# Expert weights w1 read as rows of 32 KB in two transfers of 4 MB, instead of 16 KB rows in four of 2 MB

## What is computed

```python
logits = (x @ router_w + router_b).astype(jnp.float32)
top_vals, top_idx = lax.top_k(logits, TOP_K)            # 4 of 32
gates = jax.nn.softmax(top_vals, axis=-1)
h = x_pad[tok] @ w1[e] + b1[e]                          # 1024 -> 2048
out = clamped_swiglu(h) @ w2[e] + b2[e]                 # 1024 -> 1024
out = out * row_gate[:, None]                           # then added per token
```

## Time and profile before

| | |
|---|---|
| Median of three runs | 1197.25 us (1196.84 to 1197.47) |
| Profiled execution, device time | 1195.7 us |
| Its span, first to last instruction | 1193.9 us |
| Mean granted TensorE clock | 0.963 |
| TensorE matmul busy | 1078.5 us (90%) |
| VectorE, ScalarE, GpSimd busy | 281.6, 184.7, 92.6 us |
| Moved by DMA | 429.84 MB, mean 360 GB/s |

### The profile page before, as it was taken

The page is one execution under the profiler, slowest core; times in us unless marked ns, Lnnn a source line. Parts: engine busy times, 40 slices in busy tenths (PEclk is TensorE's granted clock), DMA queues, the critical chain, the costliest instruction groups (busy, mean ns, idle before and its releaser), DMA issues.

```text
span 1193.9 us, 13476 instructions
## 1 busy us (share of the span) xinstructions
PE 1078.5 (90%) x4855; PEld 428.3 (36%) x4856; DVE 281.6 (24%) x648; ACT 184.7 (15%) x373; POOL 92.6 (8%) x133
## 2 busy tenths in 40 slices
PE   5983898999999999999999998899989998999996
PEld 4752445333333333333333333333333333333332
DVE  2997713411112111111111111111111111111112
ACT  3550611011111111111111111111111111111112
POOL 0690000000000000000000000000000000000000
PEclk9996888799999999999999999999999999999999
DMA  9800945199999996999999999999999999999981
GB/s 313 310 28 0 294 160 233 64 384 428 427 427 427 427 428 244 428 425 427 429 427 427 428 427 427 427 428 428 428 426 428 427 427 429 428 428 425 428 358 44
DMA packets 43979, 429.84 MB, mean 360 GB/s; under 512 B 6191, under 2 KB 13767, under 8 KB 19364
## 3 DMA queue, kind: packets, MB, share of 16 engines
q1 hardware_dynamic: 40492, 421.10, 84.9%
q0 software_dynamic: 3328, 8.17, 1.8%
q10 hardware_dynamic: 144, 0.38, 0.1%
HBM read 430.29 MB, written 4.62 MB: 364 GB/s over the span
## 4 chain that ended last, share of the span: by engine, by line
PE 48%; DMA 41%; DVE 8%; ACT 1%; issue 1%; SPq 0%; DVEq 0%; ACTq 0%
DMA W<-in_w_dram 41%; PE PS L926 16%; PE PS L947 15%; DVE WA L1017 3%; DVE WA L1014 3%; PE PS L811 3%; PE PS L649 2%; PE PS L918 2%; PE PS L682 1%; PE PS L645 1%; PE PS L638 1%; DMA WA<-in_state_conv_dram 1%; PE PS L620 1%; PE PS L632 1%; PE PS L867 1%
## 5 line engine op out<-in xcount | busy, mean ns | idle before, releaser
L947 PE MATMUL PS<-W,XT 128*64 128x512 f32 x1056 | 249.2, 615 | 51.4 <-DMA W<-in_w_dram 47.6
L926 PE MATMUL PS<-WB,X 128*64 128x512 f32 x1088 | 236.3, 592 | 0.0
L926 PE MATMUL PS<-WA,X 128*64 128x512 f32 x1024 | 222.4, 592 | 0.0
L1217 DVE TENSOR_SCALAR X<-PS 128x512 f32<-128x512 f32 x33 | 22.8, 691 | 607.1 <-PE PS L926 607.1
L947 PEld LDWEIGHTS PS<-W,XT 128*64 128x64 f32 x1056 | 74.7, 140 | 179.1 <-issue 122.9
L926 PEld LDWEIGHTS PS<-WB,X 128*64 128x64 f32 x1088 | 78.1, 137 | 155.3 <-issue 155.3
L926 PEld LDWEIGHTS PS<-WA,X 128*64 128x64 f32 x1024 | 73.5, 137 | 146.7 <-issue 146.7
L591 ACT ACTIVATE X<-X 128x512 f32<-128x512 f32 x33 | 20.8, 630 | 482.0 <-DVE X L1217 482.0
L1333 POOL COPY gcol<-stab 128x1 uint32 x33 | 6.0, 182 | 879.9 <-PE PS L638 879.9
L1204 DVE TENSOR_TENSOR X<-PS,par 128x512 f32<-128x512 f32 x34 | 23.5, 691 | 198.5 <-PE PS L638 198.5
L649 PE MATMUL PS<-XT 64*128 64x512 f32 x272 | 67.6, 615 | 0.0
(11 more groups left out here) (242 smaller groups left out, 657.8 us busy)
## 6 DMA issues: line engine op xcount, KB each, us to landing
WA<-in_w_dram SPq DMA_DIRECT2D x64, 2048.0 KB, 25.8
WB<-in_w_dram SPq DMA_DIRECT2D x64, 2048.0 KB, 25.2
W<-in_w_dram SPq DMA_DIRECT2D x64, 2048.0 KB, 24.7
WB<-in_w_in_dram SPq DMA_DIRECT2D x5, 1024.0 KB, 12.0
WB<-in_w_in_dram SPq DMA_DIRECT2D x1, 2048.0 KB, 14.7
W<-in_w_out_dram SPq DMA_DIRECT2D x1, 2048.0 KB, 18.4
W<-in_w_out_dram SPq DMA_DIRECT2D x2, 1024.0 KB, 9.8
h_rows<-M POOLq DMA_DIRECT2D x3, 512.0 KB, 7.5
```

What stands on the lines that cost most here:

```text
L926: last = mm(PS[64 * n:64 * n + 64, s, :], xTe[:, o:o + SLOTS], w1buf[u][:, c, q:q + 512], start=False, stop=(c == 3 and k == 1))
L947: last = mm(PS[64 * n:64 * n + 64, MIX, :], hT[:, s, h, :], w2buf[:, 4 * h + s, 512 * n:512 * n + 512], start=(s == 0 and h == 0), stop=(s ...
```

## The change

w1 is read with four neighbouring rows per partition, so a chunk has 32 KB in one run on each partition and there are two chunks of 4 MB per expert. Everything that depends on it follows: two semaphores for arrival and two for release, the order of the 64 matmuls of a block (two chunks of 32), the columns that the transposes read (every fourth element in place of every second), the layout of the router's weights, and the norm's gains, which come in one transfer of two rows and are turned by four small transposes in place of two. The first loads of the weights are cut otherwise: of w1 of expert 1, 4 MB are issued early in place of 6 MB, and 4 MB later in place of 2 MB. The bytes are the same.

```diff
-        w1buf = [WA[:, :].rearrange("p (c n) -> p c n", c=4),
-                 WB[:, :].rearrange("p (c n) -> p c n", c=4)]
+        w1buf = [WA[:, :].rearrange("p (c n) -> p c n", c=2),
+                 WB[:, :].rearrange("p (c n) -> p c n", c=2)]
...
-        w1_v = w1.rearrange("l e (c p k) n -> p (l e) c (k n)", p=P, k=2)
+        w1_v = w1.rearrange("l e (c p k) n -> p (l e) c (k n)", p=P, k=4)
...
-                (gain_rows[0:2, :], ffn_norm_g[0].rearrange("(h c n) -> h c n", h=2, c=2)[:, 0, :]),
-                (gain_rows[2:4, :], ffn_norm_g[0].rearrange("(h c n) -> h c n", h=2, c=2)[:, 1, :]),
+                (gain_rows, ffn_norm_g[0].rearrange("(h n) -> h n", h=2)),
...
-            o = 256 * chunk_of(k) + k // 4
-            return slice(o, o + 255, 2)
+            o = 512 * (k % 2) + k // 2
+            return slice(o, o + 509, 4)
...
-            load_w1(sp, 0, 0, range(2))
+            load_w1(sp, 0, 0, range(1))
...
-            load_w1(sp, 1, 1, range(3))
+            load_w1(sp, 1, 1, range(1))
...
-            load_w1(sp, 0, 0, range(2, 4))
-            load_w1(sp, 1, 1, range(3, 4))
+            load_w1(sp, 0, 0, range(1, 2))
+            load_w1(sp, 1, 1, range(1, 2))
...
-                    for c in range(4):
+                    for c in range(2):
                         sp.wait_ge(w1_used[c], end)
                         load_w1(sp, u, 2 * i + u + 2, [c])
...
-                    o = 256 * (k % 2) + k // 2
-                    last = tp(PS[:, LIN, P * k:P * k + P], xg[:, o:o + 255:2], ident)
+                    last = tp(PS[:, LIN, P * k:P * k + P], xg[:, k:k + 509:4], ident)
...
-            for k in range(2):
-                tp(PS[:, 7, 20 + 4 * k:24 + 4 * k], gain_rows[:, k::2], ident[0:4, 0:4])
+            for k in range(4):
+                tp(PS[:, 7, 20 + 2 * k:22 + 2 * k], gain_rows[:, k::4], ident[0:2, 0:2])
...
-                        for c in range(4):
+                        for c in range(2):
                             pe.wait_ge(w1_in[u][c], 16 * i + 16)
-                            for k in range(2):
-                                o = SLOTS * (4 * k + 2 * (c % 2) + c // 2)
+                            for k in range(4):
+                                o = SLOTS * (2 * k + c)
                                 for s in range(2):
                                     for n in range(2):
                                         q = 2048 * k + 1024 * s + 512 * n
                                         last = mm(PS[64 * n:64 * n + 64, s, :], xTe[:, o:o + SLOTS],
-                                                  w1buf[u][:, c, q:q + 512], start=False, stop=(c == 3 and k == 1))
+                                                  w1buf[u][:, c, q:q + 512], start=False, stop=(c == 1 and k == 3))
                             last.then_inc(w1_used[c], 1)
...
-                    dve.wait_ge(w1_used[3], m + 1)
+                    dve.wait_ge(w1_used[1], m + 1)
```

More of the change, by code:

```diff
@@ L170, in hybrid_step @@
         par_rows = c3[0:20, 3584:3712]
-        gain_rows = c3[0:4, 3712:3968]
+        gain_rows = c3[0:2, 1280:1792]
         q_sb = c3[:, 0:1280].rearrange("p (g t) -> p g t", g=G)
@@ L263, in hybrid_step @@
         kv_in, q_in, wout_in, wout2_in = (sem(n) for n in ("kv_in", "q_in", "wout_in", "wout2_in"))
-        w1_in = [[sem(f"w1_in{u}{c}") for c in range(4)] for u in range(2)]
+        w1_in = [[sem(f"w1_in{u}{c}") for c in range(2)] for u in range(2)]
         w2_in = [sem("w2_in0"), sem("w2_in1")]
@@ L278, in hybrid_step @@
         xg_ready, pool_step, xtp_ready, xT_ready = sem("xg_ready"), sem("pool_step"), sem("xtp_ready"), sem("xT_ready")
-        w1_used = [sem(f"w1_used{c}") for c in range(4)]
+        w1_used = [sem(f"w1_used{c}") for c in range(2)]
         g_ready, sig_ready = sem("g_ready"), sem("sig_ready")
@@ L293, in hybrid_step, with load_w1 @@
         nv_sv = nv_s[0].rearrange("b w h d -> b w (h d)")
-        def load_w1(eng, u, e, chunks=range(4)):
+        def load_w1(eng, u, e, chunks=range(2)):
             for c in chunks:
@@ L318, in rows_of @@
         def rows_of(k):
-            o = 256 * chunk_of(k) + k // 4
-            return slice(o, o + 255, 2)
-        def chunk_of(k):
-            return 2 * (k % 2) + k // 2 % 2
+            o = 512 * (k % 2) + k // 2
+            return slice(o, o + 509, 4)
         def Hs(i):
@@ L370, in _ @@
             sp.dma_start(sinks8, attn_sinks[0].partition_broadcast(P)).then_inc(caches_in, 16)
-            sp.dma_start(rw[:, :, :].rearrange("p (c k) e -> p c (k e)", k=2),
-                         router_w[0].rearrange("(c p k) e -> p c (k e)", p=P, k=2)).then_inc(late_in, 16)
+            sp.dma_start(rw[:, :, :].rearrange("p (c k) e -> p c (k e)", k=4),
+                         router_w[0].rearrange("(c p k) e -> p c (k e)", p=P, k=4)).then_inc(late_in, 16)
             sp.dma_start(rb[:, :], router_b[0].partition_broadcast(P)).then_inc(late_in, 16)
             sp.dma_start(b1q[:, :], b1[0].rearrange("e (q n) -> (e q) n", n=512)).then_inc(b1_in, 16)
-            load_w1(sp, 0, 0, range(2))
+            load_w1(sp, 0, 0, range(1))
             sp.dma_start(wout[:, G:KD, :], w_out[0, 512:1024, :].rearrange("(j p) n -> p j n", p=P)).then_inc(wout2_in, 16)
@@ L427, in _ @@
                 if e < E - 2:
-                    for c in range(2):
-                        sp.wait_ge(w1_used[c], end)
-                        load_w1(sp, e % 2, e + 2, [c])
+                    sp.wait_ge(w1_used[0], end)
+                    load_w1(sp, e % 2, e + 2, [0])
                 if e == E - 3:
@@ L435, in _ @@
                 if e < E - 2:
-                    for c in range(2, 4):
-                        sp.wait_ge(w1_used[c], end)
-                        load_w1(sp, e % 2, e + 2, [c])
+                    sp.wait_ge(w1_used[1], end)
+                    load_w1(sp, e % 2, e + 2, [1])
                 if e in (E - 4, E - 2):
@@ L631, in router @@
                 for k in range(KD):
-                    last = nc.tensor.matmul(PS[:, 1, E * i:E * i + E], hTr[:, k, :], rw[:, 2 * chunk_of(k) + k // 4, :], start=(k == 0), stop=(k == KD - 1))
+                    last = nc.tensor.matmul(PS[:, 1, E * i:E * i + E], hTr[:, k, :], rw[:, 4 * (k % 2) + k // 2, :], start=(k == 0), stop=(k == KD - 1))
                 last.then_inc(S["lg_done"], 1)
@@ L653, in _ @@
             pe.wait_ge(consts_in, 16)
-            pe.wait_ge(rows_in, 16 * 8)
+            pe.wait_ge(rows_in, 16 * 7)
             tp(PS[:, 7, 0:20], par_rows, ident[0:20, 0:20])
-            for k in range(2):
-                tp(PS[:, 7, 20 + 4 * k:24 + 4 * k], gain_rows[:, k::2], ident[0:4, 0:4])
+            for k in range(4):
+                tp(PS[:, 7, 20 + 2 * k:22 + 2 * k], gain_rows[:, k::4], ident[0:2, 0:2])
             for j in range(CJ):
```

## The result

The changed kernel took 1199.55 us (median of 9 runs, 1198.87 to 1201.51) against 1197.47 for the kernel before on the same chip (9 runs, 1195.79 to 1199.42). The ratio is 1.0021, with a 95% interval from 1.0011 to 1.0031: 1.3 to 3.7 us slower. The profiled execution has a span of 1197.2 us, 3.3 more than that of before.

What follows compares the result with a forecast made beforehand. Weight transfers set the pace except before two restarts of an idle queue. Terms 3.5 + 0.3 - 1.0 + 3.5 - 3.2 = +3.1 us gave 1200.3 us on the median, range 1196.8 to 1204.9.

Steps and rivals of the forecast that it cites:

- the five stretches: Start to first w1 release, seven experts' transfers, TensorE to the next release, 22 experts' transfers, two blocks; each counts in full.
- the front: Before the expert loop: two more small transposes of the gains stand ahead of the other transposes on TensorE, +0.3 us.
- The two releases: At both queue restarts w1 is released after 32 matmuls in place of 16: 3.5 us each, +7.0 us together.
- The cover behind the restart: Right behind a restart the next w1 issue has 2.4 us in hand, so the coarser release is hidden there.
- The rows of 32 KB: In w1 transfers, one 32 KB packet replaces two of 16 KB, sparing 9 ns: -1.0 and -3.2 us, -4.2 together.
- The sign of being wrong: Prediction wrong if the queue idles anywhere else, or the long stretch's slope moves by more than 0.5%.
- packets as before: Rival: rows are cut at 16 KB or priced by bytes, so only releases and front count: +7.3, 1204.6 us; chance 0.22.
- cheaper rows: Rival: 32 KB rows and fewer transfers spare more than the line says, 1196.1 or 1197.7 us, not slower; chance 0.16.
- Fewer, larger transfers: Two transfers fewer per expert on SyncE's queue: at most 2.6 us spared, taken as nothing.
- the last rival: Something at a restart or the end: a slow group, 1.7 us, or another start, 1 or 2 us either way; chance 0.08.
- Moved early loads: 2 MB of expert 1's w1 move from the issue near 121 us to that at 167, 8 us in hand: 0.
- reads at stride four: Transposes' loads at stride four cost no more than at stride two, judged from line 938: 0.

Runs made afterwards that it cites:

- the coarse release alone: Kernel before, with w1 chunks issued in pairs after 32 matmuls in place of 16, 16 KB rows and layout kept: 1204.12 us, ratio 1.0052.
- one-block pair: Kernel before and changed kernel, each with one block for every expert, the crowded expert's tokens past 64 left out: 1185.37 and 1185.03 us.
- the layout alone: Changed kernel's layout, strides and gains, but transfers, releases and early loads as in the kernel before: 1198.32 us, ratio 1.0000.
- the 8 KB rows: Changed kernel, but each w1 chunk comes in two 2 MB transfers with 8 KB runs, release still after 32 matmuls: 1213.15 us, ratio 1.0127.
- the only version here: Changed kernel's layout, first w1 chunk in two 2 MB transfers with 16 KB runs, second in one with 32 KB runs: 1197.28 us, ratio 0.9988.

## Why the prediction was right

**What bounds the kernel.** Right. The run fell apart into the five stretches of the forecast, each with the sign that was forecast.

**The time.** That the sum, 3.1, comes within 0.2 us of the difference of the two spans is in part luck: the front came out 0.56 too high by a spread that is not the change's (below), and made up for terms that came out lower. Without the front the terms make 2.4 us where 2.8 were forecast; the medians differ by 2.1. The median of 1199.55 lies just under 1199.6, up to which the forecast wanted to call a time the same; it is the interval over nine runs of each kernel that shows it slower.

**The two releases.** Right, to 0.07 us each: 3.43 and 3.43 where 3.5 and 3.5 were put. The run with the coarse release alone shows them without the long rows, the one with a release after 64 matmuls shows that they grow in proportion, and the one-block pair shows that the second hangs on the crowded expert. The cover behind the restart held too. In the changed kernel the next w1 was issued at 495.63, when the queue, at 430 GB/s, had work from 468.50 to 497.8: 2.2 us in hand where 2.4 were counted. From 250 to 452 us and from 480 to 1120 the DMA share was 1.00, so the queue idled nowhere else.

**The rows of 32 KB.** Right in kind, a little low in size: 1.20 and 3.24 us where 1.0 and 3.2 were put, 4.4 in all, and 4.7 in the pair with one block each. 4.4 us over 29 experts and 16 rows are 9.6 ns a row, against 9 from the line; the completion packets of the two transfers spared, taken as 0 to 0.5 us, are in it. The sign of being wrong that the forecast had set here, a long stretch that moves by more than 0.5%, was set too near its own forecast: the stretch is 0.49% shorter, and the bytes moved from 480 to 1120 us (273.57 and 274.97 MB) differ by 0.51%. That a row of 32 KB goes as one packet, which the trace of before could not show, the counts settle; the rival of packets as before falls with them, and that of cheaper rows was not reached.

**Fewer, larger transfers.** Right to take nothing, as far as the runs go. Of the 2 us per transfer that the Trainium skill charges (SBUF — State Buffer, "The DMA setup-cost knee") 64 transfers fewer show no trace: all that was gained is 0.15 us per expert. The row's price without a change in the number of transfers, 9.1 ns from the runs with 8 and 16 KB, accounts for 4.2 of the 4.4 us, which leaves 0.2 for all transfers spared. That is argued from shorter rows: no run has rows of 32 KB in four transfers, or two transfers with rows of 16 KB.

**The front.** The term that was mis-sized, if the two profiled executions are taken at their word: 0.86 us where 0.3 was put. The other runs say that neither number is the change's. The start of the first w1 group is at 236.31, 237.56, 238.72 and 238.65 in the four profiles with the old front, and at 237.17, 237.59, 237.40, 238.93 and 239.08 in the five with the new one. The means, 237.8 and 238.0, differ by less than either set spreads, and the kernel with the layout alone was as fast as the one before. An allowance of up to 2 us either way belonged in the forecast as the spread of the front from one execution to the next; it stood there only as a start that falls otherwise, within the last rival. What causes the spread was not tried. It begins early, at the 24 transposes of the tokens, which are the same in all nine kernels. In the kernel before, in its one-block version, whose front is the same code, and in the run with the layout alone:

```profile
16.45 3.35 PE L672 MATMUL PS<-C,WA 128*128 128x128 f32 x24
...
16.61 4.54 PE L672 MATMUL PS<-C,WA 128*128 128x128 f32 x24
...
16.74 4.61 PE L669 MATMUL PS<-C,WA 128*128 128x128 f32 x24
```

The granted clock is 1.00 from 14 to 21 us in all three, so it is not the clock that the profile shows.

**Moved early loads and reads at stride four.** Right at zero, both. The w2 issue behind the moved load stands at 195.97, 28.6 us after it; from 188 us on the DMA share was 0.18, so the load had landed. The loads at stride four took 209 ns, as at stride two; the forecast of near 200 for them, made from line 938, was not met, so the 12 ns between the two lines are not the stride's. The trace thus shows no price for the step past a 16-byte line which the Trainium skill names (SBUF — State Buffer, "Door 1: The DMA port swizzle").

**The end of the run.** The last wait came at 1126.63, forecast for 1126.4, and nothing behind it changed. The group ahead of it took 3.65 us, as in the kernel before; that was the execution's luck. The slow group of the last rival came at this very place in the profiles of the layout alone, the 8 KB rows and the release after 64 matmuls. TensorE in the layout alone, the window of that group, and the window of the same group in the changed kernel:

```profile
1121.83 5.35 PE L944 MATMUL PS<-W,XT 128*64 128x512 f32 x16 [2.58 <-DMA W<-in_w_dram]
...
1121.80:1127.20 5.40, 5.37 (x17) 1.53 (x17) 0.00 (x0) 0.00 (x0) 0.00 (x0) 0.68 1.01 428
...
1121.70:1125.40 3.70, 3.66 (x17) 1.13 (x17) 0.00 (x0) 0.00 (x0) 0.00 (x0) 1.00 1.06 456
```

The granted clock was 0.68 of full speed, a mean over its two levels (1.2 and 2.4 GHz), against 1.00, the upper one. The second half started 1.07 us later for it than in the kernel before, counted from the start of this group. What lowers the clock was not tried: the engine had waited 2.58 us here and 2.41 in the changed kernel, but a wait of 1.97 us was followed by a group of 3.65 us in the kernel before (448.12) and by one of 5.35 in the layout alone (450.39).

## What to carry to other kernels

Where a queue of transfers sets the pace, look for the moments at which it runs dry. In this kernel the size of the unit that frees a buffer was paid in full there and nowhere else, and the second such moment added to the first. Between them a longer run saves a fixed few ns per packet, here 9, which could be read from two sizes that the trace already had. The two wishes need not share a size: small pieces where a restart waits for them and long rows behind gave the only version here that was faster than both.

## What the runs showed of the hardware

The price of a packet of no length, 9 ns beside the bytes, was read from packets of 4 and 16 KB and held at 8 and 32 KB: 423, 427 and 430 GB/s with w1 in rows of 8, 16 and 32 KB, at the same DMA share. I had not expected a row of 32 KB to follow the line of the smaller ones to within a ns. A restart of the queue cost 3.2 us (3.5 with the longer rows) beyond the time that it stood idle.
